# PEER gates of a one-core decoder layer: one 256-column fp32r matmul a token, fed by single-scalar one-hots from GpSimd

## The chip, the cores and the metric

One core of one Trainium2 chip runs the whole program as one launch. The metric is the device time of that launch in microseconds (us). The kernel before took 1032.17 us (median of 3 runs, 1032.04 to 1032.56).

## What is computed

One decoder layer over 256 positions of width 1024: an attention sub-layer (three head groups, one output projection), a layer norm, then the PEER sub-layer and a second layer norm. The change lies in PEER alone. For each token, 8 retrieval heads pick 16 experts each out of 128 x 128 = 16,384, with a softmax over each head's 16 scores as gates:

```
cand_idx = i1 * 128 + i2                      # expert = (first key, second key)
gate = softmax(top_s)                         # 128 (expert, gate) pairs for each token
a = gelu(einsum('cd,ced->ce', xc, expert_u[ec]))
y = einsum('ce,ced->cd', gate * a, expert_v[ec])
```

The kernel does not gather. It computes gelu(x . u) for all 16,384 experts, multiplies by a gate matrix that is zero where a token did not choose the expert, and multiplies by all of expert_v. The gate matrix of one token is 128 x 128 (second key x first key). It is made on TensorE: with the token's 128 routing slots on the partitions, one operand is a one-hot of each slot's second key, the other a one-hot of its first key scaled by the slot's gate; their product sums over the slots.

## The kernel before, in words

**Blocks.** Experts are split by first key into NK = 128 blocks of 128 experts. The in stage runs `expert_in(c)` for c = 0 to 127: 24 matmuls of 256 columns in fp32r into PSUM bank c % 2. Both fp32 operands are split into a high fp32r part and a rest, and three products of parts are added for each of 8 slices of the width. The out stage runs `expert_out(c)` in the same manner, 12 matmuls of 512 columns a block, into banks 4 to 7. All operands of `mm` (L464) have that one line in the trace.

**The work around one block of the in stage.** SyncE loads the block's 512 KB (`load_u`, L377, one of UR = 6 buffers, the sixth in the storage of `ahl`). ScalarE makes its high part (`u_split`, L1001, three blocks ahead), VectorE its rest (`fill`, L1405: raw minus high part, both in SBUF). After the matmuls ScalarE takes the gelu from PSUM: for c < N0 = 41 straight into `arena` (L1075), later into a small buffer `gel` (L1079), which VectorE multiplies into `arena` (`block_gate`, L1609). `arena` (128 x 32768 fp32) holds activations of all experts: G[expert in block, block, token].

**The gates.** The routes (which experts, which gates) are final at about block 37; `turn_routes` turns them so that slots lie on the partitions and ScalarE saves them in `slotT` (L1089). Then the tokens are done in GN = 64 groups of four. Group g stands on TensorE in front of block N0 + g (`gates`, L850), one group a block, so the 64 groups take blocks 41 to 104. For each group:
- GpSimd makes two of the second-key one-hots (`onehots`, L445: iota compared with a scalar of the slot, 128 x 128), behind a small copy of the scalars (L440).
- ScalarE makes the third in two steps (`onehot`, L1093 and L1098).
- VectorE makes the fourth (L1584) and the four scaled first-key one-hots (L1585), 128 x 128 fp32 each.
- TensorE does four matmuls of fp32 operands with 128 columns; each shows as two MATMUL records. They fill one bank of four (`gate_bank`, GB = 4).
- VectorE multiplies the bank's 512 columns into `arena` (`gate_group`, L1599). The parts of `arena` that hold no activation yet are first filled with ones (L434 to L453, `fill_ones` L1106), so that a block's later `block_gate` multiplies the gate that is already there.

One-hots are double buffered: group g may be built once the matmuls of group g - 2 are done (`pe_g`).

**What sets the order.** Each engine has its own program, written out by hand, and works it in order; semaphores join them. VectorE's for one gated block is `fill`, `onehots(g + 1)`, `gate_group(g)`, `block_gate`. SyncE issues every load from one queue in order: u blocks, then the v blocks of the out stage (L413), the first of which waits for all 64 groups. The v buffers 4 to 7 lie over the one-hots and constants.

Of the kernel before, what the change touches and what calls it, by code (L numbers as in the profile page):

```python
# [15 lines left out]
P = 128  # L16
# [12 lines left out]
PH = 8  # L29
# [11 lines left out]
POOL_HOT = 2  # L41
GN = S // 4
UR, UH = 6, 3
VR, VH = 8, 4
GB = 4
# [37 lines left out]
K_ID, K_IOTA, K_TRI, K_CB, K_FREQ = 0, 128, 256, 512, 512 + T * NC  # L83
# [60 lines left out]
def peer_layer_kernel(nc, x, xT, memT, positions, w_tok, w_memq, w_memk, w_memv, w1k, w1v, w2k, w2v, peT,  # L144
                      w_out, ln1, wq, subk, uT, pv, ln2, consts, out):
    with ExitStack() as ctx:
# [20 lines left out]
        gel = sb("gel", [P, 2, S])  # L167

# [3 lines left out]
        n2 = sb("n2", [P, 2, 4])  # L172
        one = sb("one", [P, 1])[:, :]
        dist = sb("dist", [P, 2, P])
# [35 lines left out]
        slotT = small(3 * S).rearrange("p (a t) -> p a t", a=3)  # L210
        pe_sb = small(2 * LP).rearrange("p (a l) -> p a l", a=2)
        w2k_sb = gel[:, 1, 0:P]
        w2v_sb = gel[:, 1, P:P + HD]
        qT = gel[:, 0, :].rearrange("p (b t) -> p b t", b=2)
        subk_sb = small(2 * P).rearrange("p (a n) -> p a n", a=2)
# [89 lines left out]
        n2_ready, oh2_ready = sem("n2_ready"), sem("oh2_ready")  # L305
        hot_dist, oh3_ready = sem("hot_dist"), sem("oh3_ready")
        oh_ready, pe_g = sem("oh_ready"), sem("pe_g")
# [4 lines left out]
        ones_low, ones_high, ones_mid, one_ready = (sem(n) for n in ("ones_low", "ones_high", "ones_mid", "one_ready"))  # L312
# [19 lines left out]
        def hot(g):  # L332
            return oh[:, g % 2]

        def gate_bank(g):
            return (2, 3, 6, 7)[g % GB]

        def u_raw(c):
            b = c % UR
            return raw[:, b, :] if b < 4 else hi_raw[:, 3, :] if b == 4 else ahl_raw[:, :]  # L340

        def u_rest_of(c):
            b = c % UR
            return lo[:, b, :] if b < 4 else hi[:, 3, :] if b == 4 else ahl[:, :, :, :].rearrange("p b a t -> p (b a t)")
# [11 lines left out]
        def _(sp):  # L356
# [38 lines left out]
            for c in (0, 1, 4, 5):  # L395
                load_u(c)
# [26 lines left out]
        def _(pool):  # L423
# [7 lines left out]
            nc.gpsimd.memset(one, 1.0).then_inc(one_ready, 1)  # L431
            pool.wait_ge(q_saved, 4 * PH)
            pool.wait_ge(x1_split, 4)
            nc.gpsimd.memset(arena[:, N0 * S:A_S1], 1.0)  # L434
            nc.gpsimd.memset(arena[:, A_END:A_V], 1.0).then_inc(ones_low, 1)
            pool.wait_ge(g_shift, 2)
            nc.gpsimd.memset(arena[:, A_S1:A_EX], 1.0)

            def onehots(g):
                nc.gpsimd.tensor_copy(n2[:, g % 2, :], slotT[:, 1, 4 * g:4 * g + 4]).then_inc(n2_ready, 1)  # L440
# [7 lines left out]
            pool.wait_ge(rT_saved, T)  # L448
            onehots(0)
            onehots(1)  # L450
            nc.gpsimd.memset(arena[:, A_EX:A_R], 1.0)
            nc.gpsimd.memset(arena[:, A_V:A_ALL], 1.0)
            nc.gpsimd.memset(arena[:, A_R + 4096:A_END], 1.0).then_inc(ones_high, 1)  # L453
            for g in range(2, GN):
                onehots(g)
# [6 lines left out]
        def _(pe):  # L462
# [399 lines left out]
            for c in range(NK):  # L862
                if c == NTURN:
                    turn_routes()
                if 0 <= c - N0 < GN:
                    gates(c - N0)
                expert_in(c)
# [29 lines left out]
        def _(act):  # L897
# [188 lines left out]
            def save_routes():  # L1086
                for t in range(T):
                    act.wait_ge(pe_rT, t + 1)
                    nc.scalar.copy(slotT[:, :, t * P:(t + 1) * P],  # L1089
                                   ps[:, 2 + t, 0:3 * P].rearrange("p (a n) -> p a n", a=3)).then_inc(rT_saved, 1)  # L1090

            def onehot(g):
                nc.scalar.activation(dist[:, g % 2, :], iota, ACT.Abs, scale=-1.0,  # L1093
                                     bias=slotT[:, 1, 4 * g + POOL_HOT:4 * g + POOL_HOT + 1]).then_inc(hot_dist, 1)
                if g >= 2:
                    act.wait_ge(pe_g, g - 1)
                act.wait_ge(hot_dist, g + 1)
                nc.scalar.activation(hot(g)[:, 0, POOL_HOT, :], dist[:, g % 2, :], ACT.Relu, scale=-1.0, bias=1.0  # L1098
                                     ).then_inc(oh3_ready, 1)

            def fill_ones(part):
                n = 2048
                at = A_R + part * n
                if part == 0:
                    act.wait_ge(one_ready, 1)
                nc.scalar.copy(arena[:, at:at + n], one.to_broadcast([P, n])).then_inc(ones_mid, 1)  # L1106
# [37 lines left out]
        def _(dve):  # L1144
# [432 lines left out]

            def onehots(g):
                if g >= 2:
                    dve.wait_ge(pe_g, g - 1)  # L1580
                for q in range(4):
                    tok = slice(4 * g + q, 4 * g + q + 1)
                    if q > POOL_HOT:
                        v.tensor_scalar(hot(g)[:, 0, q, :], iota, slotT[:, 1, tok], None, ALU.is_equal)  # L1584
                    ins = v.tensor_scalar(hot(g)[:, 1, q, :], iota, slotT[:, 0, tok], slotT[:, 2, tok],  # L1585
                                          ALU.is_equal, ALU.mult)
                ins.then_inc(oh_ready, 1)

            def gate_group(g, blocks):
                dve.wait_ge(pe_g, g + 1)  # L1590
                if g == 0:
                    dve.wait_ge(ones_low, 1)
                    dve.wait_ge(ones_high, 1)
                    dve.wait_ge(ones_mid, 2)
                    dve.wait_ge(gelu_done, N0)
                if blocks:
                    dve.wait_ge(gated, blocks)
                a = G[:, :, 4 * g:4 * g + 4]
                v.tensor_tensor(a, ps[:, gate_bank(g), :].rearrange("p (q c) -> p c q", q=4), a, ALU.mult  # L1599
                                ).then_inc(pre_gated, 1)  # L1600

            def block_gate(c, groups):
                dve.wait_ge(gelu_done, c + 1)
                if groups:
                    dve.wait_ge(pre_gated, groups)
                else:
                    dve.wait_ge(ones_low, 1)
                a = arena[:, c * S:(c + 1) * S]
                v.tensor_tensor(a, gel[:, c % 2, :], a, ALU.mult).then_inc(gated, 1)  # L1609
# [4 lines left out]
            dve.wait_ge(rT_saved, T)  # L1614
            onehots(0)
            fill()
            for g in range(GN):
                fill()
                if g + 1 < GN:
                    onehots(g + 1)  # L1620
                gate_group(g, max(0, g - 2))
                if g >= 2:
                    block_gate(N0 + g - 2, g + 1)
# [5 lines left out]
            def a_split(c):  # L1629
                if c == 0:  # L1630
                    dve.wait_ge(pre_gated, GN)
                    dve.wait_ge(pe_h, NK - 2)
# [10 lines left out]
            for c in range(N0 + GN - 2, NK):  # L1643
                if filled[0] < NK:
                    fill()
                block_gate(c, GN)
                if c >= NK - 3 and c < NK - 1:
                    a_split(c - NK + 3)
                    v_rest(c - NK + 3)
# [75 lines left out]
```

## Time and profile before

| | |
|---|---|
| Median of 3 runs | 1032.17 us |
| The profiled execution's own time | 1032.03 us |
| Its span, first to last instruction | 1030.0 us |
| TensorE busy | 1016.0 us, 99% |
| VectorE, ScalarE, GpSimd busy | 72%, 42%, 10% |
| Granted TensorE clock, mean | 0.998 of full speed |

The profile lists busy time of each engine, with PE for TensorE's matmuls, PEld its weight loads, DVE for VectorE, ACT for ScalarE, POOL for GpSimd and SP for SyncE. A timeline row gives the start in us, the length in us, the engine, the line, the operation, its tiles and sizes, how many instructions it joins, and in brackets the idle time in front of it with what ended it. The time outside the span is 2.0 us.

### The profile page before, as it was taken

The page shows a single profiled execution, that of the slowest core. Times are in us where ns is not written, and L with a number is a line of the kernel's source. Part 1 is how long each engine was busy: PE and PEld are TensorE (multiplying, and loading weights), DVE is VectorE, ACT ScalarE, POOL GpSimd, SP SyncE. Part 2 cuts the span into 40 slices and gives each one's busy share as a digit, 9 for nine tenths or more (in the row PEclk, how much of TensorE's full clock was granted, in tenths as well). Part 3 has the DMA queues.
Part 4 walks back from the last instruction along what each step waited for, and adds up shares of the span by engine and source line. Part 5 has one row for each costly group of instructions (what it writes and reads, how often), then busy time and mean ns, then how long its engine had stood idle before and what let it go on. Part 6 is the DMA issues. An engine that isn't in the chain of part 4 may idle for free.

```text
span 1030.0 us, 17462 instructions
## 1 busy us (share of the span) xinstructions
PE 1016.0 (99%) x6514; PEld 894.2 (87%) x6514; DVE 742.2 (72%) x1798; ACT 432.2 (42%) x763; POOL 107.1 (10%) x210
## 2 busy tenths in 40 slices
PE   9999999999999999999999999999999999999996
PEld 3478865999999999999999999988888888888885
DVE  1165543788999679999999975566666666666667
ACT  1245432233444755555555544443333334343441
POOL 1000000004000143333333300000000000000000
PEclk9999999999999999999999999999999999999999
DMA  9742200793555544444444455576555555555551
GB/s 334 308 162 105 83 21 0 223 343 122 183 182 182 179 155 136 141 144 144 143 136 138 139 164 184 185 245 214 195 193 196 190 197 188 200 188 200 187 181 42
DMA packets 48755, 176.52 MB, mean 171 GB/s; under 512 B 5136, under 2 KB 6176, under 8 KB 47520
## 3 DMA queue, kind: packets, MB, share of 16 engines
q1 hardware_dynamic: 48272, 173.82, 49.5%
q0 software_dynamic: 400, 1.58, 0.4%
q8 instruction: 53, 0.87, 0.3%
q14 instruction: 30, 0.25, 0.1%
HBM read 174.33 MB, written 1.05 MB: 170 GB/s over the span
## 4 chain that ended last, share of the span: by engine, by line
PE 97%; DVE 1%; DMA 1%; ACT 0%; SPq 0%; issue 0%; DVEq 0%
PE ps L464 95%; PE ps L643 1%; DMA arena<-in_w_tok 1%; DVE xs L1676 0%; DVE xs L1670 0%; DVE arena L1664 0%; DVE xs L1661 0%; PE ps L683 0%; PE ps L543 0%; PE ps L712 0%; PE ps L532 0%; ACT slab L973 0%; ACT arena L969 0%; SPq L358 0%; PE ps L847 0%
## 5 line engine op out<-in xcount | busy, mean ns | idle before, releaser
L464 PE MATMUL ps<-x1hl,hi 128*128 128x256 f32 x2216 | 377.7, 285 | 0.0
L464 PEld LDWEIGHTS ps<-x1hl,hi 128*128 128x128 f32 x2216 | 327.3, 192 | 0.0
L464 PE MATMUL ps<-hi,ahl 128*128 128x512 f32 x992 | 265.3, 389 | 0.0
L1114 ACT CAST hi<-slab 128x1024 fp32r<-128x1024 f32 x128 | 135.2, 1056 | 204.6 <-PE ps L464 204.4
L464 PEld LDWEIGHTS ps<-hi,ahl 128*128 128x128 f32 x992 | 186.2, 188 | 38.6
L464 PE MATMUL ps<-x1hl,lo 128*128 128x256 f32 x688 | 194.6, 283 | 0.0
L1626 DVE TENSOR_TENSOR lo<-slab,hi 128x1024 fp32r<-128x1024 f32 x128 | 156.0, 1219 | 0.0
L464 PE MATMUL ps<-lo,ahl 128*128 128x512 f32 x496 | 152.7, 389 | 0.0
L464 PEld LDWEIGHTS ps<-x1hl,lo 128*128 128x128 f32 x688 | 131.7, 191 | 0.0
L1405 DVE TENSOR_TENSOR lo<-slab,hi 128x1024 fp32r<-128x1024 f32 x86 | 106.1, 1233 | 16.3 <-ACT hi L1001 16.2
L464 PE MATMUL ps<-arena 128*128 128x128 f32 (+6 forms) x806 | 111.6, 293 | 1.9 <-DVE arena L1156 1.4
L1001 ACT CAST hi<-slab 128x1024 fp32r<-128x1024 f32 x107 | 111.3, 1040 | 0.0
L1639 DVE CAST ahl<-arena 128x256 fp32r<-128x256 f32 x124 | 36.4, 294 | 102.5 <-PE ps L464 102.5
L464 PEld LDWEIGHTS ps<-arena 128*128 128x128 f32 (+2 forms) x806 | 98.3, 192 | 13.6 <-issue 8.2
L464 PEld LDWEIGHTS ps<-lo,ahl 128*128 128x128 f32 x496 | 93.1, 188 | 19.2
L1079 ACT ACTIVATE gel<-ps 128x256 f32<-128x256 f32 x87 | 33.4, 384 | 146.8 <-PE ps L464 146.8
L464 PE MATMUL ps<-arena,slab 128*128 128x512 f32 (+2 forms) x256 | 92.0, 503 | 1.8 <-ACT slab L973 1.4
L445 POOL TENSOR_SCALAR slab<-slab,n 128x128 f32<-128x128 f32 x128 | 78.0, 622 | 151.3 <-PE ps L464 151.1
L464 PE MATMUL ps<-slab 128*128 128x128 f32 (+1 forms) x576 | 86.0, 289 | 0.0
L464 PEld LDWEIGHTS ps<-arena,slab 128*128 128x128 f32 x256 | 44.9, 190 | 43.4 <-issue 39.4
L1585 DVE TENSOR_SCALAR slab<-slab 128x128 f32<-128x128 f32 x256 | 76.1, 337 | 0.0
L464 PEld LDWEIGHTS ps<-slab 128*128 128x128 f32 x576 | 73.5, 192 | 0.6
(201 smaller groups left out, 822.9 us busy)
## 6 DMA issues: line engine op xcount, KB each, us to landing
slab<-in_pv SPq DMA_DIRECT2D x128, 512.0 KB, 3.3
slab<-in_uT SPq DMA_DIRECT2D x107, 512.0 KB, 3.3
arena<-in_wq SPq DMA_DIRECT2D x32, 512.0 KB, 5.7
ahl_raw<-in_uT SPq DMA_DIRECT2D x21, 512.0 KB, 3.3
arena<-in_w_tok SPq DMA_DIRECT2D x2, 2048.0 KB, 16.7
arena<-in_w_out SPq DMA_DIRECT2D x1, 4096.0 KB, 13.3
arena<-in_w_tok SPq DMA_DIRECT2D x4, 512.0 KB, 8.3
arena<-in_w_tok SPq DMA_DIRECT2D x1, 1792.0 KB, 19.0
```

The costliest lines, as they stand in the source:

```text
L445: ins = nc.gpsimd.tensor_scalar(hot(g)[:, 0, q, :], iota, n2[:, g % 2, q:q + 1], None, ALU.is_equal)
L464: return nc.tensor.matmul(o, lhsT, rhs, start=start, stop=stop, skip_group_check=True)
L643: last = nc.tensor.transpose(ps[:, 2, b * P:(b + 1) * P], xb[u % 3][:, b * P:(b + 1) * P], ident)
L1001: nc.scalar.copy(hi[:, c % UH, :], u_raw(c)).then_inc(u_hi, 1)
L1079: nc.scalar.activation(gel[:, c % 2, :], ps[:, c % 2, 0:S], ACT.Gelu).then_inc(gelu_done, 1)
L1114: nc.scalar.copy(hi[:, v_hi_slot(c), :], raw[:, v_slot(c), :]).then_inc(v_hi, 1)
L1405: v.tensor_tensor(u_rest_of(c), u_raw(c), hi[:, c % UH, :].bitcast(F32), ALU.subtract).then_inc(u_lo, 1)
L1585: ins = v.tensor_scalar(hot(g)[:, 1, q, :], iota, slotT[:, 0, tok], slotT[:, 2, tok], ALU.is_equal, ALU.mult)
L1626: v.tensor_tensor(lo[:, v_slot(c), :], raw[:, v_slot(c), :], hi[:, v_hi_slot(c), :].bitcast(F32), ALU.subtract).then_inc(v_lo, 1)
L1639: v.tensor_copy(o[:, 0, :], a).then_inc(a_hi, 1)
```

## The change

The gate matmuls take fp32r operands, 256 columns a token: the gate of each slot is split into a high part and a rest, and `pair` holds the first-key one-hot scaled by the one and by the other, side by side. `hot2` is the second-key one-hot. The two products lie side by side in PSUM (two banks a group, three groups in flight) and VectorE adds them with a reduction out of PSUM. GpSimd makes seven one-hots with a single scalar each: three unscaled first-key ones and the four second-key ones. ScalarE scales the three by both parts (six copies), VectorE makes the pair of token 0 of each group with one instruction. The 64 groups are stretched over blocks 41 to 123, 16 groups in 21 blocks (`GROUP_AT`). Blocks that are not done yet receive the gate by a plain write (second reduction), so the fills with ones are gone; done ones are multiplied; `gelu` and `block_gate` of a block handle the tokens gated so far (`gated_by`). u blocks have five buffers instead of six.

```diff
-UR, UH = 6, 3
+UR, UH = 5, 3
-GB = 4
+GB = 3
+DVE_PAIR, ACT_PAIR = (0,), (1, 2, 3)
+GROUP_AT = [N0 + g * 21 // 16 for g in range(GN)]
...
+        hot2 = nc.alloc_sbuf_tensor_at("hot2", [P, 2, 4, P], F32R, offset=ahl_at)
+        pair = nc.alloc_sbuf_tensor_at("pair", [P, 2, 4, 2, P], F32R, offset=slab_at + 4 * 4096)
+        tbl = slab[:, 8320 - 4 * S:8320].rearrange("p (t a) -> p t a", a=4)
+        low = slab[:, 6144 + P:6144 + P + 8 * P].rearrange("p (b c q) -> p b c q", b=2, q=4)
...
+        def gate_banks(g):
+            return slice(2 + 2 * (g % GB), 4 + 2 * (g % GB))
+        def gated_by(c):
+            return 4 * sum(at_ <= c for at_ in GROUP_AT)
...
@@ SyncE @@
-            for c in (0, 1, 4, 5):
+            for c in (0, 1, 4):
                 load_u(c)
...
                 if c == 0:
                     sp.wait_ge(pe_g, GN)
+                elif c == 2:
+                    sp.wait_ge(pre_gated, GN)
                 elif 4 <= c < VR:
-                    sp.wait_ge(pe_h, (NK - 1, NK, NK - 5, NK - 4)[c - 4])
+                    sp.wait_ge(pe_h, (NK - 2, NK - 1, NK, NK - 4)[c - 4])
...
@@ GpSimd @@
             def onehots(g):
                 if g >= 2:
                     pool.wait_ge(pe_g, g - 1)
-                pool.wait_ge(n2_ready, g + 1)
-                for q in range(POOL_HOT):
-                    ins = nc.gpsimd.tensor_scalar(hot(g)[:, 0, q, :], iota, n2[:, g % 2, q:q + 1], None, ALU.is_equal)
-                ins.then_inc(oh2_ready, 1)
+                for q in ACT_PAIR:
+                    ins = nc.gpsimd.tensor_scalar(pair[:, g % 2, q, 1, :], iota, tbl[:, 4 * g + q, 0:1], None, ALU.is_equal)
+                ins.then_inc(pool_first, 1)
+                for q in range(4):
+                    ins = nc.gpsimd.tensor_scalar(hot2[:, g % 2, q, :], iota, tbl[:, 4 * g + q, 1:2], None, ALU.is_equal)
+                ins.then_inc(pool_hot, 1)
+            pool.wait_ge(table_ready, 1)
+            for g in range(GN):
                 onehots(g)
...
@@ TensorE @@
             def gates(g):
-                pe.wait_ge(oh_ready, g + 1)
-                pe.wait_ge(oh2_ready, g + 1)
-                pe.wait_ge(oh3_ready, g + 1)
+                pe.wait_ge(dve_hot, g + 1)
+                pe.wait_ge(act_hot, g + 1)
+                pe.wait_ge(pool_hot, g + 1)
                 if g >= GB:
                     pe.wait_ge(pre_gated, g - GB + 1)
+                banks = ps[:, gate_banks(g), :]
                 for q in range(4):
-                    last = mm(ps[:, gate_bank(g), q * P:(q + 1) * P], hot(g)[:, 0, q, :], hot(g)[:, 1, q, :],
-                              q == 0, True)
+                    last = mm(banks[:, q // 2, (q % 2) * S:(q % 2 + 1) * S], hot2[:, g % 2, q, :],
+                              pair[:, g % 2, q, :, :].rearrange("p a n -> p (a n)"), q % 2 == 0, True)
                 last.then_inc(pe_g, 1)
...
@@ ScalarE @@
             def gelu(c):
                 act.wait_ge(pe_h, c + 1)
+                n = gated_by(c)
+                if n:
                     if c >= N0 + 2:
                         act.wait_ge(gated, c - N0 - 1)
+                    ins = nc.scalar.activation(gel[:, c % 2, 0:n], ps[:, c % 2, 0:n], ACT.Gelu)
+                if n < S:
+                    ins = nc.scalar.activation(arena[:, c * S + n:(c + 1) * S], ps[:, c % 2, n:S], ACT.Gelu)
+                ins.then_inc(gelu_done, 1)
+            def pairs(g):
+                act.wait_ge(pool_first, g + 1)
+                for q in ACT_PAIR:
+                    nc.scalar.activation(pair[:, g % 2, q, 0, :], pair[:, g % 2, q, 1, :].bitcast(F32), ACT.Copy,
+                                         scale=tbl[:, 4 * g + q, 2:3]).then_inc(act_lows, 1)
+                for n, q in enumerate(ACT_PAIR):
+                    act.wait_ge(act_lows, len(ACT_PAIR) * g + n + 1)
+                    ins = nc.scalar.activation(pair[:, g % 2, q, 1, :], pair[:, g % 2, q, 1, :].bitcast(F32), ACT.Copy,
+                                               scale=tbl[:, 4 * g + q, 3:4])
+                ins.then_inc(act_hot, 1)
             for c in range(NK):
                 gelu(c)
+                if c == NTURN:
+                    pairs(0)
+                for g in range(1, GN):
+                    if GROUP_AT[g] == c + 2:
+                        pairs(g)
+                if c + UH < NK:
+                    u_split(c + UH)
...
@@ VectorE @@
+            def tables():
+                dve.wait_ge(rT_saved, T)
+                did(v.tensor_copy(tbl[:, :, 3].bitcast(F32R), tbl[:, :, 2]))
+                settle()
+                v.tensor_tensor(tbl[:, :, 2], tbl[:, :, 2], tbl[:, :, 3], ALU.subtract).then_inc(table_ready, 1)
             def onehots(g):
                 if g >= 2:
                     dve.wait_ge(pe_g, g - 1)
+                for q in DVE_PAIR:
+                    ins = v.scalar_tensor_tensor(out=pair[:, g % 2, q, :, :], in0=iota.unsqueeze(1).to_broadcast([P, 2, P]),
+                                                 scalar=tbl[:, 4 * g + q, 0:1],
+                                                 in1=tbl[:, 4 * g + q, 2:4].unsqueeze(2).to_broadcast([P, 2, P]),
+                                                 op0=ALU.is_equal, op1=ALU.mult)
+                ins.then_inc(dve_hot, 1)
+            def gate_group(g):
+                k = GROUP_AT[g]
+                both = ps[:, gate_banks(g), :].rearrange("p b (q a c) -> p c (b q) a", q=2, a=2)
+                a = G[:, :, 4 * g:4 * g + 4]
+                both_low = low[:, g % 2]
+                dve.wait_ge(pe_g, g + 1)
+                did(v.tensor_reduce(both_low[:, 0:k, :], both[:, 0:k, :, :], AX_X, ALU.add))
+                v.tensor_reduce(a[:, k:NK, :], both[:, k:NK, :, :], AX_X, ALU.add)
+                settle()
+                dve.wait_ge(gelu_done, k)
+                v.tensor_tensor(a[:, 0:k, :], both_low[:, 0:k, :], a[:, 0:k, :], ALU.mult).then_inc(pre_gated, 1)
+            def block_gate(c):
+                n = gated_by(c)
+                dve.wait_ge(gelu_done, c + 1)
+                dve.wait_ge(pre_gated, n // 4)
+                a = arena[:, c * S:c * S + n]
+                v.tensor_tensor(a, gel[:, c % 2, 0:n], a, ALU.mult).then_inc(gated, 1)
...
+            for c in range(N0, NK + 1):
                 if filled[0] < NK:
                     fill()
+                for g in range(1, GN):
+                    if GROUP_AT[g] == c + 1:
+                        onehots(g)
+                for g in range(GN):
+                    if GROUP_AT[g] == c:
+                        gate_group(g)
+                if c > N0:
+                    block_gate(c - 1)
```

## Rows read from the trace of the kernel before

**Rows 1.** The page: busy time of TensorE and VectorE; the chain that ended last, by engine and line.
```profile
PE 1016.0 (99%) x6514; PEld 894.2 (87%) x6514; DVE 742.2 (72%) x1798; ACT 432.2 (42%) x763; POOL 107.1 (10%) x210
...
PE 97%; DVE 1%; DMA 1%; ACT 0%; SPq 0%; issue 0%; DVEq 0%
```

**Rows 2.** Two stretches: us, busy PE, PEld, DVE, ACT, POOL; PEclk, DMA share, GB/s.
```profile
355.00:603.00 248.00, 248.00 (x2108) 248.00 (x2107) 228.62 (x510) 130.57 (x265) 90.61 (x195) 1.00 0.43 143
603.50:660.00 56.50, 56.50 (x473) 56.50 (x472) 34.13 (x43) 25.60 (x39) 0.00 (x0) 1.00 0.58 190
```

**Rows 3.** Timeline of one gated block, ScalarE, GpSimd and VectorE.
```profile
399.30 0.38 ACT L1079 ACTIVATE gel<-ps 128x256 f32<-128x256 f32 x1 [1.74 <-PE ps L464]
399.58 1.04 ACT L1001 CAST hi<-slab 128x1024 fp32r<-128x1024 f32 x1
...
400.25 1.18 POOL L445 TENSOR_SCALAR slab<-slab,n 128x128 f32<-128x128 f32 x2 [2.45 <-PE ps L464]
400.51 0.41 ACT L1093 ACTIVATE dist<-slab 128x128 f32<-128x128 f32 x1
400.98 0.49 DVE L1609 TENSOR_TENSOR arena<-gel,arena 128x256 f32<-128x256 f32 x1
401.01 0.31 ACT L1098 ACTIVATE slab<-dist 128x128 f32<-128x128 f32 x1
401.38 0.19 POOL L440 COPY n<-slab 128x4 f32<-128x4 f32 x1
401.40 1.25 DVE L1405 TENSOR_TENSOR lo<-slab,hi 128x1024 fp32r<-128x1024 f32 x1
402.57 0.85 DVE L1585 TENSOR_SCALAR slab<-slab 128x128 f32<-128x128 f32 x3
403.06 0.38 ACT L1079 ACTIVATE gel<-ps 128x256 f32<-128x256 f32 x1 [1.74 <-PE ps L464]
```

**Rows 4.** Timeline of blocks without gates, and the last gelu of the in stage.
```profile
609.34 0.39 ACT L1079 ACTIVATE gel<-ps 128x256 f32<-128x256 f32 x1 [1.56 <-PE ps L464]
...
612.22 0.38 ACT L1079 ACTIVATE gel<-ps 128x256 f32<-128x256 f32 x1 [1.56 <-PE ps L464]
...
672.70 0.38 ACT L1079 ACTIVATE gel<-ps 128x256 f32<-128x256 f32 x1 [1.56 <-PE ps L464]
```

**Rows 5.** `block_gate` with gates (first) and without (second): ns min/median/max.
```profile
L1609 DVE TENSOR_TENSOR arena<-gel,arena x60: 425/492/494, 374.6 to 596.9; 128x256 f32<-128x256 f32 x60
...
L1609 DVE TENSOR_TENSOR arena<-gel,arena x26: 418/426/426, 604.4 to 673.1; 128x256 f32<-128x256 f32 x26
```

**Rows 6.** Timeline, first groups: VectorE and GpSimd at once.
```profile
354.58 1.23 DVE L1405 TENSOR_TENSOR lo<-slab,hi 128x1024 fp32r<-128x1024 f32 x1 [1.66 <-ACT hi L1001]
...
355.37 0.48 POOL L440 COPY n<-slab 128x4 f32<-128x4 f32 x1 [37.34 <-ACT slab L1089]
...
355.95 1.30 POOL L445 TENSOR_SCALAR slab<-slab,n 128x128 f32<-128x128 f32 x2
...
366.35 2.23 POOL L445 TENSOR_SCALAR slab<-slab,n 128x128 f32<-128x128 f32 x2 [4.16 <-PE ps L464]
...
366.90 1.22 DVE L1405 TENSOR_TENSOR lo<-slab,hi 128x1024 fp32r<-128x1024 f32 x1
...
370.12 2.23 POOL L445 TENSOR_SCALAR slab<-slab,n 128x128 f32<-128x128 f32 x2 [1.39 <-PE ps L464]
```

**Rows 7.** VectorE's groups of the whole span: the nearest to the new operations.
```profile
L1542 DVE TENSOR_REDUCE arena<-arena 128x32 f32<-128x1600 f32 x4 | 7.3, 1814 | 0.0
...
L1240 DVE SCALAR_TENSOR_TENSOR xs<-arena,slab,xs 128x256 f32<-128x256 f32 x7 | 3.4, 484 | 0.7
...
L1318 DVE TENSOR_REDUCE slab<-ps 128x2 f32<-128x512 f32 x4 | 2.8, 689 | 0.9 <-PE ps L464 0.8
```

**Rows 8.** Landing of the u blocks (the page, DMA issues).
```profile
slab<-in_uT SPq DMA_DIRECT2D x107, 512.0 KB, 3.3
```

**Rows 9.** GpSimd's one-hots of the whole span: ns min/median/max.
```profile
L445 POOL TENSOR_SCALAR slab<-slab,n x128: 603/605/1649, 356.0 to 596.7; 128x128 f32<-128x128 f32 x128
```

More of the change, by code:

```diff
@@ L79 @@
         NLEAD = NCAND
-K_ID, K_IOTA, K_TRI, K_CB, K_FREQ = 0, 128, 256, 512, 512 + T * NC
+K_IOTA, K_ID, K_TRI, K_CB, K_FREQ = 0, 128, 256, 512, 512 + T * NC
 K_ALL = K_FREQ + 12
@@ L171, in peer_layer_kernel @@
         sm = slab[:, 6144 + K_ALL:8320]
-        n2 = sb("n2", [P, 2, 4])
-        one = sb("one", [P, 1])[:, :]
-        dist = sb("dist", [P, 2, P])
         lnst = sb("lnst", [P, T, 8])
@@ L209, in peer_layer_kernel @@
         gcoef = small(16)
-        slotT = small(3 * S).rearrange("p (a t) -> p a t", a=3)
         pe_sb = small(2 * LP).rearrange("p (a l) -> p a l", a=2)
+        assert at[0] <= 8320 - 6144 - K_ALL - 4 * S
+        tbl = slab[:, 8320 - 4 * S:8320].rearrange("p (t a) -> p t a", a=4)
         w2k_sb = gel[:, 1, 0:P]
@@ L304, in peer_layer_kernel @@
         pe_rT, rT_saved = sem("pe_rT"), sem("rT_saved")
-        n2_ready, oh2_ready = sem("n2_ready"), sem("oh2_ready")
-        hot_dist, oh3_ready = sem("hot_dist"), sem("oh3_ready")
-        oh_ready, pe_g = sem("oh_ready"), sem("pe_g")
+        table_ready = sem("table_ready")
+        pool_first, pool_hot = sem("pool_first"), sem("pool_hot")
+        act_lows, act_hot = sem("act_lows"), sem("act_hot")
+        dve_hot, pe_g = sem("dve_hot"), sem("pe_g")
         u_in = [sem(f"u_in{b}") for b in range(UR)]
@@ L311, in peer_layer_kernel @@
         pe_h, gelu_done, pre_gated, gated = sem("pe_h"), sem("gelu_done"), sem("pre_gated"), sem("gated")
-        ones_low, ones_high, ones_mid, one_ready = (sem(n) for n in ("ones_low", "ones_high", "ones_mid", "one_ready"))
         a_hi, a_lo, pe_y = sem("a_hi"), sem("a_lo"), sem("pe_y")
@@ L429, in _ @@
             pool.dma_start(subk_sb, subk).then_inc(l_sk, 16)
[L431 to L437, printed above, removed]
             def onehots(g):
-                nc.gpsimd.tensor_copy(n2[:, g % 2, :], slotT[:, 1, 4 * g:4 * g + 4]).then_inc(n2_ready, 1)
                 if g >= 2:
                     pool.wait_ge(pe_g, g - 1)
-                pool.wait_ge(n2_ready, g + 1)
-                for q in range(POOL_HOT):
-                    ins = nc.gpsimd.tensor_scalar(hot(g)[:, 0, q, :], iota, n2[:, g % 2, q:q + 1], None, ALU.is_equal)
-                ins.then_inc(oh2_ready, 1)
[L448 to L454, printed above, removed]
+                for q in ACT_PAIR:
[6 more added lines that the diff above has]
+            for g in range(GN):
                 onehots(g)
@@ L864, in _ @@
                     turn_routes()
-                if 0 <= c - N0 < GN:
-                    gates(c - N0)
+                for g in range(GN):
+                    if GROUP_AT[g] == c:
+                        gates(g)
                 expert_in(c)
@@ L1088, in save_routes @@
                     act.wait_ge(pe_rT, t + 1)
-                    nc.scalar.copy(slotT[:, :, t * P:(t + 1) * P],
+                    nc.scalar.copy(tbl[:, t * P:(t + 1) * P, 0:3].rearrange("p t a -> p a t"),
                                    ps[:, 2 + t, 0:3 * P].rearrange("p (a n) -> p a n", a=3)).then_inc(rT_saved, 1)
[L1092 to L1106, printed above, removed]
+            def pairs(g):
[8 more added lines that the diff above has]
+                ins.then_inc(act_hot, 1)
             def v_split(c):
@@ L1575, in _ @@
                                 ).then_inc(route_ready, 1)
+            def tables():
[3 more added lines that the diff above has]
+                v.tensor_tensor(tbl[:, :, 2], tbl[:, :, 2], tbl[:, :, 3], ALU.subtract).then_inc(table_ready, 1)
+                dve.wait_ge(table_ready, 1)
             def onehots(g):
@@ L1580, in onehots @@
                     dve.wait_ge(pe_g, g - 1)
[L1581 to L1589, printed above, removed]
-                dve.wait_ge(pe_g, g + 1)
[L1591 to L1600, printed above, removed]
@@ L1602, in block_gate @@
-            def block_gate(c, groups):
-                dve.wait_ge(gelu_done, c + 1)
[L1604 to L1609, printed above, removed]
+                for q in DVE_PAIR:
[3 more added lines that the diff above has]
+                                                 op0=ALU.is_equal, op1=ALU.mult)
@@ L1613, in _ @@
                 fill()
-            dve.wait_ge(rT_saved, T)
+            tables()
             onehots(0)
             fill()
[L1617 to L1623, printed above, removed]
+            fill()
+            assert filled[0] == N0 + 1
             def v_rest(c):
@@ L1631, in a_split @@
                     dve.wait_ge(pre_gated, GN)
-                    dve.wait_ge(pe_h, NK - 2)
                 if c >= N0:
@@ L1641, in a_split @@
                 v.tensor_tensor(o[:, 1, :], a, o[:, 0, :].bitcast(F32), ALU.subtract).then_inc(a_lo, 1)
-            for c in range(N0 + GN - 2, NK):
+            for c in range(N0, NK + 1):
                 if filled[0] < NK:
                     fill()
[L1646 to L1649, printed above, removed]
+                for g in range(1, GN):
+                    if GROUP_AT[g] == c + 1:
+                        onehots(g)
+                for g in range(GN):
+                    if GROUP_AT[g] == c:
+                        gate_group(g)
+                if c > N0:
+                    block_gate(c - 1)
+                if NK - 2 <= c < NK:
+                    a_split(c - NK + 2)
+                    v_rest(c - NK + 2)
             for c in range(2, NK):
```

23 lines of the change are left out of this document (3 added, 20 removed).

## The prediction, made before the changed kernel was run

> **What bounds the kernel now.** I began with the page's busy times and its chain. TensorE is busy for 99% of the span and holds 97% of the chain [rows 1], so a microsecond counts only if TensorE loses it or is made to wait for it. The windows then show where gates are made: from 355 to 603 us TensorE is busy without a gap, VectorE for 229 of 248 us, ScalarE for 131, GpSimd for 91 with its waits between groups left out. After that TensorE is as full and VectorE has room again [rows 2]. The clock granted is full, 2.4 GHz, in both. The timeline gives the price of a gate group: the gelus of successive blocks stand 3.76 us apart with a group between them [rows 3], 2.88 us without [rows 4]. A group costs TensorE 0.88 us, so eight records of 0.11 us, and one of the 24 matmuls of 256 columns of a block costs 2.88 / 24 = 0.12 us.
>
> The profiled execution took 1032.0 us for a span of 1030.0; the median of the runs shown is 0.1 us higher. A measurement of this kernel tells about 0.2%, 2 us, from no change.
>
> **TensorE's part.** Four matmuls of 256 columns, fp32r like those of a block, cost 4 x 0.12 = 0.48 us a group. 64 x (0.88 - 0.48) = 26 us less, if nobody makes TensorE wait. Stretching the groups moves this work, it adds none: 16 groups in 21 blocks are 21 x 2.88 + 16 x 0.48 = 68.2 us, or 4.26 us a group. That is the time within which every other engine must make a group.
>
> **VectorE.** An operation of n elements costs about 0.15 us + 1.05 ns an element, from 0.43 us for 256 [rows 5] and 1.22 for 1024 [rows 6], and starts 0.08 before its forerunner ends. A fill: 1.17 from start to start [rows 3]. The pair of token 0 (256 elements): 0.48 [rows 7], so 0.40. The reductions read 1024 elements: 1600 take 1.81 us and 512 out of PSUM 0.69 [rows 7], 1.03 ns each; two of them and the wait behind them make 1.3. The multiply into the done blocks has 4k elements, k from 41 to 123: 0.25 to 0.59. `block_gate` has up to 256: 0.1 to 0.35. In the last 21 blocks that is 16 x (0.40 + 1.3 + 0.55) + 21 x (1.17 + 0.31) = 67 us, just under 68.2; in the first 21 it is 59. VectorE fits, with about 1 us of cover at the end. If the cover is gone, it costs a few us.
>
> **ScalarE.** 21 blocks: a high part at 0.94 and the gelu in two halves at some 0.36, so 27 us; six scaled copies of 128 columns a group at 0.31 to 0.41 each [rows 3], 30 to 39 us. 57 to 66 us fit in 68.2, and most of the duration of a copy lies beside the next one. Behind `pairs(g)` waits a high part needed two blocks later; it follows GpSimd's first three one-hots, so it is late only if GpSimd is.
>
> **Loads.** With five buffers a u block is asked for two blocks, 5.8 us, ahead of its high part; it lands in 3.3 us [rows 8]. I cost it at nothing, hidden by TensorE's blocks. The first v block now waits for the group in front of block 123 and is used after block 127, some 14 us on: nothing. The dropped fills with ones and the split of the gates (two short operations on VectorE) lie beside blocks 37 to 41: nothing.
>
> **GpSimd is where I differ from that sum.** It makes seven one-hots a group. Two of them take 1.13 us from the first's start to the next instruction's [rows 3], 0.565 each, so seven take 3.96 us. Alone they would fit in 4.26 with 0.3 to spare. They aren't alone. In rows 6 the same pair takes 2.23 us, twice; the first time, whose VectorE row stands there too, a fill starts during it: 366.90 + 1.22 = 368.12, and the pair is done 0.46 later. The 0.19 us copy takes 0.48 beside the fill that ends at 355.81 and is itself done at 355.85. GpSimd was held until VectorE's instruction ended, for 1.05 us of 1.22. Nearly all other pairs of the kernel before escaped it only by their place: they run beside `gate_group` and `block_gate` and end as the fill starts [rows 3]. In the changed kernel GpSimd works without pause, and 84 fills stand in 84 blocks.
>
> The price of a fill: GpSimd asks once in 0.565 us; the loss is 1.05 at worst and 1.05 - 0.565 = 0.49 at best, 0.77 on average. With 1.31 fills a group that is 1.01 us (0.64 to 1.38).
>
> For `block_gate`, the multiply and the pair instruction no row shows GpSimd held. Rows 5 show that `block_gate` and GpSimd touch: 0.492 us beside it, 0.426 alone. All three read two operands in SBUF, as the fill does; `gate_group` before and the new reductions read PSUM and have no second SBUF tensor. So I bound them: nothing if only long instructions hold GpSimd; 1.10 us a group if all their time counts (0.28 + 0.42 + 0.40). Met singly, each at half its length times its chance to be met, they would cost 0.35. They are written back to back with the fill (multiply, `block_gate`, fill, pair), so I take 0.90, near the upper end.
>
> **The sum.** A group takes GpSimd 3.96 + 1.01 + 0.90 = 5.87 us instead of TensorE's 4.26. It starts about 0.4 us after it did, at 356.3 [rows 6], and behind its last group come 0.5 us of matmuls, five blocks of 2.88 and 0.2 to the last gelu: 356.3 + 64 x 5.87 + 15.1 = 747.1 us. That gelu stands at 672.7 now [rows 4]. The out stage is untouched, so the kernel becomes 74.4 us longer: 1106 us. The even point is 64 groups in 301.3 us, 4.71 us each: a loss of 0.75 us a group, all causes together.
>
> The Trainium skill, SBUF — State Buffer, sections on SBUF's two sides and on who interferes with whom, states that VectorE with two SBUF inputs and a GpSimd instruction that reads SBUF exclude each other for a whole instruction, and that a reduction never does. That agrees with rows 6. It would count the three shorter instructions too; by rows 6 alone, with fills only, the sum is 356.3 + 64 x 4.97 + 15.1 = 689.5, 1049 us.
>
> **The rivals.**
> 1. GpSimd isn't held enough to matter; TensorE stays the bound. For it: 3.96 is below 4.26, and the one-hots before had a median of 0.605 us [rows 9]. Against it: the ones of rows 6. It gives 1032 - 26 = 1006 us, up to 1010 with VectorE's thin cover. It decides if the loss a group stays under 0.3 us, a quarter of a us a fill. Chance 0.08.
> 2. Only fills hold GpSimd: 1049 us, and 1025 to 1072 by the bounds of a fill (group 4.60 to 5.34). The short lower end of this is still faster. Chance 0.12.
> 3. TensorE, waiting in every group, is given the lower clock of 1.2 GHz. Its waits would be 1.6 us a group, and it has had no such rhythm of waits before: the clock stood at full in every stretch of rows 2. At half speed a group's share is 1.31 x 5.76 + 0.96 = 8.5 us, 64 of them 545 us, some 1280 us in all. Chance 0.03.
> 4. The forecast, GpSimd held by all four kinds: group 4.95 (0.64 + 0.35) to 6.44 (1.38 + 1.10), so 1048 to 1143 us. Chance 0.77.
>
> **The numbers.** The likeliest case gives 1106. The range runs from 1046 to 1143: it holds nearly all of the forecast's case and the upper half of the fills-only one, and leaves out full speed and the slow clock. Faster by over 0.2%: 0.08 + 0.02 = 0.10; within: 0.02; slower: 0.88.
>
> **What would show it.** GpSimd busy in nearly all of the gated stretch, its one-hots with a median of about 0.6 us and about one in five or six over 1 us, ending just behind a fill. TensorE's idle time released by GpSimd, 80 to 120 us of it, the groups spaced 5.3 us at first and over 6 late (the multiply grows with k). Gate matmuls of 0.12 us. VectorE and ScalarE less busy a microsecond than before, the fills at 1.22 us still, `block_gate` waiting for gates. I am wrong if one-hots stay at 0.6 us beside fills, if TensorE's waits name VectorE or ScalarE, or if the in stage ends before 672.7 us.

## The result: slower by 4.85%, with GpSimd as the bound of the gated stretch

The changed kernel took 1082.07 us (median of 4 runs, 1081.78 to 1082.99) against 1032.11 before: a ratio of 1.0485, 95% interval 1.0467 to 1.0503. The prediction was 1106 us with a range of 1046 to 1143.

From the page after (busy times, slices of the span, the chain that ended last, groups), which answer to [rows 1] and [rows 9]:

```profile
PE 1001.8 (93%) x6258; PEld 872.2 (81%) x6258; DVE 746.1 (69%) x1672; ACT 505.8 (47%) x1099; POOL 352.1 (33%) x459
...
PE   9999999999999987878888787899999999999996
...
POOL 1000000000000699999999999910000000000000
PEclk9999999999999999999999999999999999999999
...
PE ps L456 64%; POOL hot L442 17%; POOL pair L439 15%; PE ps L635 1%; DVE xs L1670 0%; DVE xs L1664 0%; DVE arena L1658 0%; DVE xs L1655 0%; PE ps L675 0%; ACT hi L995 0%; PE ps L535 0%; PE ps L524 0%; PE ps L704 0%; DVE hi L1395 0%; ACT slab L1085 0%
...
L439 POOL TENSOR_SCALAR pair<-slab 128x128 fp32r<-128x128 f32 x192 | 162.0, 856 | 354.6 <-DVE slab L1572 354.0
...
L442 POOL TENSOR_SCALAR hot<-slab 128x128 fp32r<-128x128 f32 x256 | 188.3, 749 | 0.0
```

GpSimd works from within slice 14 to the end of slice 26, and TensorE has its only large gap there. 32% of the chain runs through GpSimd's two lines; before, TensorE alone had 97%. The mean one-hot takes 0.86 us (L439) and 0.75 us (L442). The clock stays at full speed.

First the waits from 355 to 730 us (us in total, times, longest), then the gated stretch as a whole (us, busy PE, PEld, DVE, ACT, POOL; PEclk, DMA share, GB/s), answer to [rows 2]:

```profile
ACT pair L1091 <- POOL pair L439: 73.1, 43, 3.3
DVE lo L1395 <- ACT hi L995: 69.7, 48, 4.5
PEld ps L456 <- issue: 69.5, 42, 2.0
PE ps L456 <- POOL hot L442: 59.8, 39, 1.9
```
```profile
359.00:707.00 348.00, 283.95 (x2276) 276.42 (x2274) 261.97 (x418) 227.19 (x634) 347.31 (x448) 1.00 0.39 129
```

GpSimd works 347 of 348 us. TensorE loses 64 us there, most of it to the last of the second-key one-hots; ScalarE waits for the first-key ones, and the fills wait for ScalarE behind it. VectorE and ScalarE have a quarter and a third of the stretch free.

The timeline of a held one-hot and what held it (GpSimd and VectorE), to be read beside [rows 6]:

```profile
499.59 1.23 DVE L1395 TENSOR_TENSOR hi<-slab,hi 128x1024 fp32r<-128x1024 f32 x1 [1.57 <-ACT hi L995]
...
499.87 2.00 POOL L439 TENSOR_SCALAR pair<-slab 128x128 fp32r<-128x128 f32 x2
500.74 0.76 DVE L1591 TENSOR_REDUCE slab<-ps 128x292 f32<-128x584 f32 x1
501.41 0.61 DVE L1592 TENSOR_REDUCE arena<-ps 128x220 f32<-128x440 f32 x1
501.85 3.26 POOL L442 TENSOR_SCALAR hot<-slab 128x128 fp32r<-128x128 f32 x4
501.94 0.59 DVE L1595 TENSOR_TENSOR arena<-slab,arena 128x292 f32<-128x292 f32 x1
502.45 0.27 DVE L1602 TENSOR_TENSOR arena<-gel,arena 128x100 f32<-128x100 f32 x1
502.64 1.31 DVE L1395 TENSOR_TENSOR lo<-slab,hi 128x1024 fp32r<-128x1024 f32 x1
```

Two one-hots that take 1.18 us alone take 2.00 when the first begins 0.28 us into a fill. The reductions of 500.74 and 501.41 run beside the second and hold nothing.

I took every one of the 448 one-hots of this trace, subtracted the median duration of 0.600 us, and put what was left to the VectorE instruction that ended 0.39 to 0.48 us before the one-hot did:

| VectorE instruction | one-hots held | us in all | us a group |
|---|---|---|---|
| fill L1395 | 83 | 69.9 | 1.09 |
| multiply of the done blocks L1595 | 35 | 11.0 | 0.17 |
| `block_gate` L1602 | 39 | 6.6 | 0.10 |
| pair L1579 | 1 | 0.3 | 0.00 |
| reductions L1591, L1592 | 0 | 0 | 0 |

An unheld one-hot starts 0.580 us after the last. So a group is 7 x 0.58 + 1.09 + 0.17 + 0.10 = 5.42 us; from the first start at 358.59 to the last end at 707.19 it is 348.6 / 64 = 5.45. The last gelu, which ended the in stage at 672.70 [rows 4], stands here:

```profile
722.59 0.39 ACT L1072 ACTIVATE gel<-ps 128x256 f32<-128x256 f32 x1 [1.56 <-PE ps L456]
```

722.6 - 672.7 = 49.9 us, and the kernel is 50.0 us longer: all of the loss lies in front of this gelu.

### The profile page after: what moved, and what is told of

The parts are those of the page before. It is cut to its first block, busy times and chain, and to the rows that moved or that the text cites. A ratio compares the mean times of both kernels' runs of the same rounds, so it can differ in the third digit from the quotient of the medians.

```text
span 1080.0 us, 17285 instructions
## 1 busy us (share of the span) xinstructions
PE 1001.8 (93%) x6258; PEld 872.2 (81%) x6258; DVE 746.1 (69%) x1672; ACT 505.8 (47%) x1099; POOL 352.1 (33%) x459
## 4 chain that ended last, share of the span: by engine, by line
PE 66%; POOL 31%; DVE 1%; ACT 1%; issue 0%; DVEq 0%; ACTq 0%
PE ps L456 64%; POOL hot L442 17%; POOL pair L439 15%; PE ps L635 1%; DVE xs L1670 0%; DVE xs L1664 0%; DVE arena L1658 0%; DVE xs L1655 0%; PE ps L675 0%; ACT hi L995 0%; PE ps L535 0%; PE ps L524 0%; PE ps L704 0%; DVE hi L1395 0%; ACT slab L1085 0%
## 5 line engine op out<-in xcount | busy, mean ns | idle before, releaser
L456 PEld LDWEIGHTS ps<-x1hl,hi 128*128 128x128 f32 x2248 | 331.0, 192 | 2.5 <-DVE lo L1395 2.5
L439 POOL TENSOR_SCALAR pair<-slab 128x128 fp32r<-128x128 f32 x192 | 162.0, 856 | 354.6 <-DVE slab L1572 354.0
L456 PE MATMUL ps<-x1hl,lo 128*128 128x256 f32 x824 | 233.7, 284 | 0.0
L1106 ACT CAST hi<-slab 128x1024 fp32r<-128x1024 f32 x128 | 135.3, 1057 | 204.5 <-PE ps L456 204.4
L442 POOL TENSOR_SCALAR hot<-slab 128x128 fp32r<-128x128 f32 x256 | 188.3, 749 | 0.0
L1395 DVE TENSOR_TENSOR lo<-slab,hi 128x1024 fp32r<-128x1024 f32 x103 | 128.7, 1251 | 79.5 <-ACT hi L995 79.4
L456 PEld LDWEIGHTS ps<-x1hl,lo 128*128 128x128 f32 x824 | 158.8, 193 | 0.0
L1614 DVE TENSOR_TENSOR lo<-slab,hi 128x1024 fp32r<-128x1024 f32 x128 | 156.0, 1219 | 0.0
L995 ACT CAST hi<-slab 128x1024 fp32r<-128x1024 f32 x128 | 133.1, 1040 | 0.0
L456 PE MATMUL ps<-pair,hot 128*128 128x256 f32 x256 | 44.1, 294 | 62.2 <-POOL hot L442 59.8
L1091 ACT ACTIVATE pair<-pair,slab 128x128 fp32r<-128x128 f32 x192 | 63.4, 397 | 73.1 <-POOL pair L439 73.1
L456 PEld LDWEIGHTS ps<-pair,hot 128*128 128x128 f32 x256 | 34.5, 189 | 69.5 <-issue 69.5
```

Of the source, the lines that this page charges most:

```text
L439: ins = nc.gpsimd.tensor_scalar(pair[:, g % 2, q, 1, :], iota, tbl[:, 4 * g + q, 0:1], None, ALU.is_equal)
L442: ins = nc.gpsimd.tensor_scalar(hot2[:, g % 2, q, :], iota, tbl[:, 4 * g + q, 1:2], None, ALU.is_equal)
L456: return nc.tensor.matmul(o, lhsT, rhs, start=start, stop=stop, skip_group_check=True)
L995: nc.scalar.copy(hi[:, c % UH, :], u_raw(c)).then_inc(u_hi, 1)
L1091: nc.scalar.activation(pair[:, g % 2, q, 0, :], pair[:, g % 2, q, 1, :].bitcast(F32), ACT.Copy, scale=tbl[:, 4 * g + q, 2:3]).then_inc(act ...
L1106: nc.scalar.copy(hi[:, v_hi_slot(c), :], raw[:, v_slot(c), :]).then_inc(v_hi, 1)
```

## The experiments

**Theory:** a VectorE instruction that reads two operands in SBUF keeps GpSimd from reading until it ends. **Rivals:** every long VectorE instruction does; one-hots are simply slower in company, each by the same share; GpSimd is innocent, and VectorE or ScalarE ran out of time. The kernel before took 1032.3 us beside each run. Runs 1 to 8 are one execution each; the repeated executions of a kernel in this case lie within 2 us of each other. Runs 1 to 4 leave out a part of the computation: they tell time only.

**1. Take the second operand away, keep the length.** The subtraction of the high part is left out of the fills from block 42 on.

```diff
-v.tensor_tensor(u_rest_of(c), u_raw(c), hi[:, c % UH, :].bitcast(F32), ALU.subtract)
+v.tensor_reduce(u_rest_of(c), u_raw(c).unsqueeze(2), AX_X, ALU.add)
```

> Fills from block 42 on become a reduction over an axis of one: the same 1024 elements at about 1.2 us, the same output, but one SBUF input; the subtraction of the high part is left out there. Theory (two SBUF operands of VectorE hold GpSimd): no one-hot is held by a fill any more, a group takes 7 x 0.58 + 0.28 = 4.34 us, the stretch becomes 1.1 us a group shorter, 1082 - 70 = 1012 us. Rival (any long VectorE instruction on SBUF, or the writes, hold it): 1.09 us a group stays, 1080 to 1083 us.

Measured: 1013.5 us. VectorE's groups (first line) and GpSimd's:

```profile
L1397 DVE TENSOR_REDUCE lo<-slab 128x1024 fp32r<-128x1024 f32 x69 | 83.5, 1210 | 16.5 <-ACT hi L995 16.5
```
```profile
L442 POOL TENSOR_SCALAR hot<-slab 128x128 fp32r<-128x128 f32 x256 | 157.5, 629 | 0.0
L439 POOL TENSOR_SCALAR pair<-slab 128x128 fp32r<-128x128 f32 x192 | 122.6, 652 | 356.5 <-DVE slab L1576 353.9 <-PE ps L456 2.5
```

The fill is as long as ever, 1.21 us, it writes the same place, and it holds nothing: the one-hots are back at 0.63 and 0.65 us, and 68.5 us of the time are gone. "Any long instruction" falls, and so does any cause in the output or in the number of one-hots. `block_gate` now met 66 one-hots for 12.5 us and the pair 15 for 2.3 us; something else is met when the fill isn't.

**2. One operand, but the faster copy.** The same fills as a cast, the subtraction left out again.

```diff
+v.tensor_copy(u_rest_of(c), u_raw(c)).then_inc(u_lo, 1)
```

> The same fills become a plain cast of the raw block: one SBUF input, fp32, shorter (0.69 us for 1024 elements in the kernel before), the subtraction left out. Theory in its narrow form (only two operands hold): no hold, as the reduction, 1012 us. Theory in its wide form, in which VectorE's faster copy uses GpSimd's way to SBUF as well: each cast holds for 0.69 us, a loss of about 0.69 - 0.29 = 0.40 a fill, 0.5 us a group, 1044 us. Rival of any long instruction: the same 1044, so this run is read together with the reduction.

Measured: 1051.9 us. VectorE's groups (first line), then GpSimd's:

```profile
L1396 DVE CAST lo<-slab 128x1024 fp32r<-128x1024 f32 x69 | 51.6, 748 | 73.0 <-ACT hi L995 73.0
```
```profile
L442 POOL TENSOR_SCALAR hot<-slab 128x128 fp32r<-128x128 f32 x256 | 181.8, 724 | 0.0
L439 POOL TENSOR_SCALAR pair<-slab 128x128 fp32r<-128x128 f32 x192 | 138.7, 735 | 354.6 <-DVE slab L1575 353.8 <-PE ps L456 0.8
```

A fill shorter by 0.46 us than the reduction makes the kernel 38 us slower than the reduction does. The cast reads one tensor, yet it holds GpSimd: 82 one-hots that end just behind a cast are 0.5 us too long on average. So two operands are sufficient, not necessary: this fp32 copy, which does 1024 elements in 0.75 us where the reduction takes 1.21, holds too, and in one respect more tightly. Of the 82, 35 end 0.38 to 0.47 us behind the cast, as they do behind a fill. The other 47 had begun before the cast and end 0.14 us behind it; no one-hot ends that closely behind a fill of two operands. One of the 47, and its cast:

```profile
375.97 1.05 POOL L439 TENSOR_SCALAR pair<-slab 128x128 fp32r<-128x128 f32 x1
376.01 0.87 DVE L1396 CAST hi<-slab 128x1024 fp32r<-128x1024 f32 x1 [0.57 <-ACT hi L995]
```

In the changed kernel 76 one-hots had begun 0.1 us or more before a fill, and 75 ended ahead of it. Here as many had begun 0.1 us or more before a cast, and 42 ended behind it, among them all that had begun less than 0.29 us before. So a cast costs 0.5 us and not the 0.40 expected. The Trainium skill, SBUF — State Buffer, section "Who interferes with whom", says that copies and casts in a two-port mode contend with GpSimd, and that a reduction never does. Runs 1 and 2 agree with both, though only its 0.75 us speak for this cast being in such a mode.

**3. Six one-hots instead of seven.** The second-key one-hot of each group's last token is left stale.

```diff
-for q in range(4):
+for q in range(4 if g < 2 else 3):
     ins = nc.gpsimd.tensor_scalar(hot2[:, g % 2, q, :], iota, tbl[:, 4 * g + q, 1:2], None, ALU.is_equal)
```

> GpSimd makes six one-hots a group instead of seven; the second-key one-hot of the group's last token is left stale. Theory (a loss per fill, not per one-hot): a group is 0.58 us shorter, 64 x 0.58 = 37 us, 1045 us. Rival (each one-hot is slower in company, 5.45 / 7 = 0.78 us each): 64 x 0.78 = 50 us, 1032 us.

Measured: 1046.8 us, 35.3 us less, which over the 62 groups with six one-hots is 0.57 a group: the bare 0.58 of a one-hot. The loss belongs to the fill, not to the one-hot; by the same reckoning as above, 83 one-hots were held by fills for 71.3 us. "Slower by a share" (1032) falls.

**4. Two one-hots, to lift GpSimd off the path.** Five of seven are left stale from group 2 on.

```diff
-for q in ACT_PAIR:
+for q in (ACT_PAIR if g < 2 else (1,)):
...
-for q in range(4):
+for q in range(4 if g < 2 else 1):
```

> GpSimd makes two one-hots a group, the other five stay stale. GpSimd then needs 2 x 0.58 + 1.37 = 2.5 us a group, far below TensorE's 4.26. If VectorE and ScalarE fit as the prediction costed them, TensorE is the bound again: 1006 to 1010 us, which is what the matmuls alone bring. If VectorE is over its budget late in the stretch (its busy time came to 4.3 us a group there), 1012 to 1020.

Measured: 1010.2 us. Two stretches, early and late, columns as in [rows 2]:

```profile
380.00:440.00 60.00, 60.00 (x503) 60.00 (x502) 49.14 (x91) 48.84 (x139) 26.60 (x28) 1.00 0.51 165
...
560.00:620.00 60.00, 60.00 (x503) 60.00 (x502) 56.32 (x93) 50.51 (x142) 31.94 (x28) 1.00 0.51 165
```

TensorE is full in both; VectorE goes from 49 to 56 of 60 us and does not run out (57.9 of 60 in the last stretch, 580 to 640 us). This is what the change is worth without GpSimd: 22.1 us, of the 26 of the matmuls.

The trace shows one thing more. In 16 groups a one-hot waited through a fill and the pair behind it, 1.18 us on average, such as this one:

```profile
389.53 1.21 DVE L1395 TENSOR_TENSOR lo<-slab,hi 128x1024 fp32r<-128x1024 f32 x1
389.95 1.57 POOL L439 TENSOR_SCALAR pair<-slab 128x128 fp32r<-128x128 f32 x1 [1.35 <-PE ps L456]
390.67 0.47 DVE L1579 SCALAR_TENSOR_TENSOR pair<-slab 128x256 fp32r<-128x256 f32 x1
```

**5. Cut each fill in two.**

```diff
+for n0 in (0, 512):
+    ins = v.tensor_tensor(u_rest_of(c)[:, n0:n0 + 512], u_raw(c)[:, n0:n0 + 512],
+                          hi[:, c % UH, n0:n0 + 512].bitcast(F32), ALU.subtract)
```

> Each fill is done in two instructions of 512 elements (0.69 us each) that still read two SBUF operands. Theory (GpSimd is held until the instruction ends, and gets in between two): a loss of about 0.69 - 0.29 = 0.40 for each half, 0.80 a fill, against 0.84 for the whole: 1.05 us a group instead of 1.09, so 3 us less at most, 1079; if GpSimd does not always land in the second half, 1065 to 1075. Rival (GpSimd is shut out for the whole time in which VectorE has two operands to read): unchanged or a little longer, 1082 to 1090.

Measured: 1078.2 us, the number of the theory, but not by its mechanism; it is 3.8 us below the changed kernel. The halves held 89 one-hots, one a fill and not two, for 66.1 us, 0.74 each. From the timeline:

```profile
565.88 2.49 POOL L439 TENSOR_SCALAR pair<-slab 128x128 fp32r<-128x128 f32 x3
...
566.11 1.29 DVE L1396 TENSOR_TENSOR lo<-slab,hi 128x512 fp32r<-128x512 f32 x2 [2.02 <-ACT hi L995]
```

Three one-hots take 2.49 us where three take 0.58 + 0.58 + 0.60 = 1.76; the middle one alone takes 1.33 and ends about 0.4 us after the second half does. In 79 of the 86 split fills GpSimd isn't let in between the two halves; in the other 7 it is, and the second half is then 0.09 us longer.

**6. Share GpSimd's work.** GpSimd keeps five one-hots; VectorE makes the second-key one-hot of token 2, ScalarE that of token 3 as |iota - s| and relu(1 - d).

```diff
+DVE_HOT = (2,)
-for q in range(4):                                     # GpSimd
+for q in (0, 1):
...
+for q in DVE_HOT:                                      # VectorE, onehots
+    ins = v.tensor_scalar(hot2[:, g % 2, q, :], iota, tbl[:, 4 * g + q, 1:2], None, ALU.is_equal)
...
+nc.scalar.activation(dist[:, g % 2, :], iota, ACT.Abs, scale=-1.0,      # ScalarE, pairs
+                     bias=tbl[:, 4 * g + 3, 1:2]).then_inc(hot_dist, 1)
...
+act.wait_ge(hot_dist, g + 1)
+nc.scalar.activation(hot2[:, g % 2, 3, :], dist[:, g % 2, :], ACT.Relu, scale=-1.0, bias=1.0)
```

> Two of GpSimd's seven one-hots move: one to VectorE (a single-scalar compare, 0.2 us from start to start), one to ScalarE (two operations, 0.6 us). GpSimd: 5 x 0.58 + 1.37 = 4.27 us a group, as much as TensorE's 4.26. VectorE gets to 4.5 and ScalarE to 4.2. Theory: TensorE and VectorE share the bound, 1008 to 1022 us, faster than the kernel before. Rival (one-hots on VectorE or the order on ScalarE cost more than their length): over 1032.

Measured: 1021.2 us, and the same kernel again, timed:

> The kernel in which GpSimd makes five one-hots, VectorE one more and ScalarE one more, timed against the kernel before. From its one look (1021.2 us beside 1032.25): 1020 to 1023 us, a ratio of 0.989, with an interval that leaves out 1. If that look was a lucky one, 1025 to 1032.

1021.46 us (1020.53 to 1022.3, 4 runs) beside 1032.32: a ratio of 0.9897, interval 0.988 to 0.9913. It beats the kernel before by 1.0% and the changed one by 61 us. Its stretches, and what TensorE waited for in it:

```profile
380.00:440.00 60.00, 60.00 (x485) 58.55 (x484) 52.84 (x102) 52.37 (x161) 56.36 (x67) 1.00 0.48 158
560.00:620.00 60.00, 58.21 (x477) 57.25 (x476) 59.26 (x102) 52.94 (x160) 56.09 (x69) 1.00 0.45 151
```
```profile
PE ps L459 <- DVE hot L1591: 3.8, 8, 0.8
PE ps L459 <- DVE lo L1402: 2.6, 1, 2.6
```

GpSimd is off the chain and VectorE is next: 59 of 60 us late in the stretch. Run 4 leaves 11 us below this.

**7. Add the two products in PSUM.** Eight fp32r matmuls of 128 columns a group; VectorE copies the part of blocks not done and multiplies the done part, both straight from PSUM.

```diff
-last = mm(banks[:, q // 2, (q % 2) * S:(q % 2 + 1) * S], hot2[:, g % 2, q, :],
-          pair[:, g % 2, q, :, :].rearrange("p a n -> p (a n)"), q % 2 == 0, True)
+for a in range(2):
+    last = mm(banks[:, q * P:(q + 1) * P], hot2[:, g % 2, q, :], pair[:, g % 2, q, a, :], q == 0 and a == 0, a == 1)
...
-did(v.tensor_reduce(both_low[:, 0:k, :], both[:, 0:k, :, :], AX_X, ALU.add))
-v.tensor_reduce(a[:, k:NK, :], both[:, k:NK, :, :], AX_X, ALU.add)
+v.tensor_copy(a[:, k:NK, :], both[:, k:NK, :])
...
-v.tensor_tensor(a[:, 0:k, :], both_low[:, 0:k, :], a[:, 0:k, :], ALU.mult)
+v.tensor_tensor(a[:, 0:k, :], both[:, 0:k, :], a[:, 0:k, :], ALU.mult)
```

> The two products of a token are added in PSUM: eight fp32r matmuls of 128 columns a group instead of four of 256. VectorE reads 512 elements in two instructions and the multiply has one SBUF operand only. GpSimd keeps seven one-hots. Theory: only the multiply's hold goes, 0.17 us a group, 11 us, so 1071 us; TensorE's gate matmuls are hidden behind GpSimd, and their duration is to be read: 0.06 us each would keep 0.48 a group, 0.12 each would make 0.96. Rival (VectorE's load as such slows GpSimd): more, below 1060.

Measured: 1064.4 us, 17.7 less instead of 11. The multiply, with PSUM for one operand, held no one-hot, and `block_gate` behind it met one, for 0.03 us (0.17 + 0.10 a group, 64 times, is 17).

**8. As 7, with VectorE's new room used:** it makes two pairs and one second-key one-hot, GpSimd five.

```diff
-DVE_PAIR, ACT_PAIR = (0,), (1, 2, 3)
+DVE_PAIR, ACT_PAIR = (0, 1), (2, 3)
+DVE_HOT = (3,)
```

> As the run before, and VectorE, freed of some 1.0 us a group, makes two pairs and one second-key one-hot. GpSimd: 5 x 0.58 + 1.09 + 0.10 = 4.1 us a group; VectorE 4.3 - 1.0 + 0.7 = 4.0; ScalarE two pairs, 2.9. Theory: TensorE is the bound. With matmuls of 0.06 us 1006 to 1010 us; with 0.12 us, 21 x 2.88 + 16 x 0.96 = 75.8 a stretch of 21 blocks, 1036. Rival (pairs on VectorE hold GpSimd as fills do, 2 x 0.2 to 0.4 us): a group of 4.5 to 4.9, 1022 to 1048.

Measured: 1033.6 us. The window late in the stretch and eight gate matmuls of one group; below, from the changed kernel, four of 256 columns:

```profile
560.00:620.00 60.00, 60.00 (x509) 60.00 (x509) 47.67 (x98) 38.29 (x102) 56.29 (x67) 1.00 0.45 150
...
602.07 1.01 PE L457 MATMUL ps<-pair,hot 128*128 128x128 f32 x8
```
```profile
505.87 0.64 PE L456 MATMUL ps<-pair,hot 128*128 128x256 f32 x4
```

TensorE is full and nobody else is: 128 columns in fp32r cost 0.11 us each, as much as a record of the fp32 matmuls before (0.11) and nearly as much as 256 columns (0.12). Half the columns save nothing, so this version gives the whole gain back on TensorE. The pairs do hold GpSimd here (63 one-hots, 0.33 us each), though GpSimd still keeps up.

## Why the prediction was right, and which term was off

- **TensorE's part**: 26 us. Right; the gate matmuls stand 0.12 us apart, and run 4 gives 22 with the rest fitting.
- **VectorE and ScalarE fit**: right. With GpSimd lifted off, TensorE is full to the end of the stretch. I costed VectorE at 67 of 68.2 us late, 98%; run 4 shows 57.9 of 60 busy from 580 to 640 us, 96%.
- **Loads, fills with ones**: costed at nothing; TensorE's waits in the stretch name no load.
- **GpSimd's bare work**: 3.96 us a group from a spacing of 0.565; it is 4.06, from 0.58. I had it from pairs in front of a copy, which begins 1.13 us after the pair does; in a run of one-hots each starts 0.58 after the last.
- **Its start**: 356.3 expected, 358.6 measured. The split of the gates on VectorE, which my paragraph on loads put at nothing, is in front of everything GpSimd does: VectorE was in a fill from 356.27, and the two operations then ran from 357.42 to 358.48. 2.3 us.
- **A fill**: 1.01 us a group against 1.09 measured (0.77 a fill against 0.84). Right.
- **The step that failed** is the 0.90 us a group for the multiply, `block_gate` and the pair. It measured 0.28. I took them near their upper end because they are written back to back with the fill, so that GpSimd would be shut out for the whole chain. It wasn't: the table has its waits end with each of these instructions, not with the chain. In the changed kernel the pair even gave way, 0.59 us at the median against 0.485 at its shortest. My own figure for meeting them singly, 0.35, was the better one. The fear was not baseless: in run 4 the same fill and pair did shut GpSimd out together, 16 times.

With the measured terms, 5.42, and 0.03 us a group of waits the sum is 358.6 + 64 x 5.45 + 15.1 = 722.5, the gelu at 722.6. Of the 24 us by which the forecast was too long, 40 are the 0.62 a group of the failed step, less 6 for the bare work, 5 for the fills and 2 for the start, and 2 for waits between groups. So part of the nearness is luck: terms that were too small gave back some 15 of the 40 us.

Two of the signs failed with that step. I expected 80 to 120 us of idle time on TensorE; it was 64. I expected groups 5.3 us apart at first and over 6 late, as the multiply grows; GpSimd's groups stand 5.40 us apart in the first half and 5.50 in the second.

Rival 1 (not held enough) fell: the loss was 1.39 us a group against its 0.3. Rival 2 (fills only) was the nearest in size, as fills are 80% of the held time. It lay at 1049, 1072 at most, and it is false in mechanism: the multiply and `block_gate` held 74 one-hots. Rival 3 fell: with waits of up to 2 us in TensorE the clock stayed at full speed.

**What stays open** is when GpSimd gets in between two VectorE instructions. Between fill and pair it always did in the changed kernel (63 times), and in run 4, with the same two instructions, 27 times; 16 times it waited through both. In all 16 the fill had begun right behind another VectorE instruction; whenever VectorE had been idle before the fill, GpSimd got in (21 times). But it also got in 6 times without that, and between the halves of run 5 only 7 times in 86. So the kinds of the two instructions don't decide it alone, and no run here tells what does.

## What to carry to other kernels

Before an engine that looks idle is given work, look in the trace for the few places where it already ran beside its neighbour: two pairs of one-hots at 2.23 us instead of 1.18, out of 64, held the whole result. Cost the new work at its bare length plus at most one wait for every neighbour's instruction that excludes it, and count those instructions, not the busy share: here nearly every fill was met (83), but only 74 of some 140 multiplies and `block_gate`s. And see which operand form the neighbour uses: the same 1024 elements cost GpSimd 1.09 us a group with two SBUF operands and none through a reduction with one.

## What I had not expected of the hardware

- GpSimd is held by a VectorE cast with a single fp32 input (run 2), by 38 us more over the kernel than by a longer reduction. The cast also holds one-hots that had begun before it.
- Two VectorE instructions of 512 elements, one right behind the other, mostly kept GpSimd out as one of 1024 did (run 5: 79 of 86 times, 0.74 us a fill against 0.84).
- An fp32r matmul of 128 columns takes 0.11 us, one of 256 columns 0.12 (runs 7 and 8, and the changed kernel).
